# Expert stage of a decoder step: u and v rows gathered apart, v one pick to a partition and a tile later

## The chip, the cores and the metric

The kernel runs on one core of a Trainium2 chip. The metric is the device time of one execution in microseconds (us), the median of several runs.

## The reference, cut to what matters

One step of a hybrid decoder layer over 1024 prompt tokens and 32 sample tokens (8 sequences of 4), all in fp32. Sliding-window attention, a gated convolution and their merge come first. The change lies in the last part, the expert layer (PEER), on the normed rows h2 of width 1024:

```python
q = (tb @ w_pq).reshape(128, 8, 2, 128)                 # 8 heads, 2 halves
s = einsum('thpd,hpkd->thpk', q, sub_keys)              # 128 keys for each half
sv, si = top_k(s, 16)
cand = sv[:, :, 0, :, None] + sv[:, :, 1, None, :]      # 16 x 16 pairs
cs, ci = top_k(cand, 16)
e = i1 * 128 + i2                                       # 16 experts of 16384, a head and token
g = softmax(cs)
a = gelu(einsum('td,thkd->thk', tb, u[e]))
out = einsum('thkd,thk->td', v[e], g * a)
```

So each of 1056 tokens reads 128 rows of u and 128 rows of v (its picks), each row 1024 fp32 (4 KB), and y = x1 + gt2 * out.

## The kernel before, in words

The table uv holds u and v of an expert side by side (8 KB). In `peer_stage` tokens lie on partitions, in 8 tiles of 128 and a ninth of 32. A unit is one tile and one head: 16 picks for each token. The loops (`schedule`) run over tiles t and heads h, and each engine works through the same units in order.

- GpSimd (`unit`, L1501) issues 16 indirect gathers a unit. One gather fetches for pick j the uv row of each of the 128 tokens, 128 x 8 KB = 1 MB, into one of the 8 buffers of `ring`. It waits on `slot_free`, which TensorE raises when it has used the buffer.
- VectorE (`dots`, L1642) multiplies the u half with `h2c` and sums along the row, one pick an instruction. After each 4 picks it makes the gelu polynomial (L1645 to L1649), takes the tanh of ScalarE (L1521) and makes 4 coefficients (L1651, L1653).
- ScalarE (`weigh`, L1525) makes a 128 x 128 diagonal of each coefficient column.
- TensorE (L1589) multiplies each diagonal with the v half, in two chunks of 512 columns, into `acc`, over all 128 picks of a tile. An fp32 matmul is recorded as two passes, so a pick is 4 records.
- The choice of experts runs one tile (8 units) ahead: TensorE makes q (L1570), its transposes (L1575) and scores (L1581), ScalarE moves them (L1532), and VectorE takes the top 16 (`choose`, L1663 to L1690) and the ids and gates (`choose_ids`, L1700 to L1714). On VectorE `choose` stands behind the 16 dots of a unit.
- Before tile 0 stands a pass `tile(-1, ...)` with the choice for its 8 units. After tile 7 the 32 sample tokens are folded: their 128 picks lie on 4 groups of 32 partitions, so that two units of 16 gathers do them. `end` multiplies `acc` with gt2 and adds x1 (L1630, L1632).

## Time and profile before

| | |
|---|---|
| median of 3 runs | 4851.54 us (4840.93 to 4852.66) |
| span of the profiled execution | 4831.2 us |
| what the median run has over this span | 20.3 us |
| busy: TensorE, VectorE, ScalarE, GpSimd | 3823.7, 2615.1, 796.5, 1264.0 us |
| DMA, whole span | 1258.73 MB, mean 261 GB/s |

The span reaches from the first to the last instruction of the profiled execution; the time of a run counts what lies around it too, and the profiled execution has no time of its own beside its span. A granted TensorE clock of 1.00 is 2.4 GHz, 0.50 is 1.2 GHz. DMA share is the mean busy share of the core's 16 DMA engines. The expert stage takes the last two thirds of the span.

### The profile page before, as it was taken

To read this page: it belongs to the slowest core of one execution; us is meant where nothing else is said; L and a number is where in the kernel's file an instruction comes from. 1 tells how busy PE (TensorE), PEld (TensorE's weight loads), DVE (VectorE), ACT (ScalarE), POOL (GpSimd) and SP (SyncE) were. 2 spreads that over 40 slices of the span, in tenths; PEclk is the share of its full clock that TensorE was granted. 3 is DMA by queue.
4 is the path that set the end of the run, shared out by engine and by line. 5 is a ranking of instruction groups with operands and counts; after the bars stand their busy time and mean duration, and the time that the engine had idled before them with its cause. 6 is when DMAs were issued, how large, how long until landed. Compare 5 with 4: busy or idle time off the path is not lost.

```text
span 4831.2 us, 47220 instructions
## 1 busy us (share of the span) xinstructions
PE 3823.7 (79%) x12534; PEld 2194.0 (45%) x12534; DVE 2615.1 (54%) x6696; ACT 796.5 (16%) x2303; POOL 1264.0 (26%) x1255
## 2 busy tenths in 40 slices
PE   7788869999997677777777777777777777777776
PEld 1455559999963333333333333333333333333331
DVE  0344442223323766666666666666666666666655
ACT  0233321112001111111111111111111111111110
POOL 0111120000000133333333333333333333333333
PEclk9888859999998888888898988898999888988888
DMA  6100011111364588988898988898998898998887
GB/s 239 66 11 9 4 49 67 62 66 63 120 226 156 202 352 346 363 346 352 357 359 346 361 353 358 353 363 344 356 364 357 337 368 349 360 353 341 323 337 286
DMA packets 201700, 1258.73 MB, mean 261 GB/s; under 512 B 27375, under 2 KB 38367, under 8 KB 64479
## 3 DMA queue, kind: packets, MB, share of 16 engines
q0 software_dynamic: 152064, 1107.36, 57.8%
q1 hardware_dynamic: 49562, 150.46, 8.8%
q8 instruction: 36, 0.59, 0.0%
q14 instruction: 38, 0.31, 0.0%
HBM read 1226.81 MB, written 32.93 MB: 261 GB/s over the span
## 4 chain that ended last, share of the span: by engine, by line
PE 21%; DVE 20%; DMA 16%; issue 8%; ACT 1%; POOL 1%; DVEq 1%; POOLq 0%; SPq 0%
PE acc_peer L1589 20%; DMA rows<-in_uv,idx 16%; DVE rows L1642 5%; POOL rows L1501 1%; DVE pick L1700 1%; DVE pick L1703 1%; DVE picked L1705 1%; DVE key_scores_rest L1667 1%; DVE top_keys L1666 1%; DVE top_keys L1673 1%; DVE pair_scores_rest L1682 1%; DVE best_scores L1684 1%; DVE best_scores L1679 1%; DVE best_pairs L1687 1%; ACT tanh L1521 1%
## 5 line engine op out<-in xcount | busy, mean ns | idle before, releaser
L1589 PE MATMUL acc_peer<-rows,diag 128*128 128x512 f32 (+1 forms) x4224 | 2146.1, 667 | 764.5 <-ACT diag L1525 764.1
L1642 DVE CUSTOM_DVE_ANT_0 rows<-rows,h_now 128x1024 f32<-128x1024 f32 x1056 | 1268.3, 1224 | 926.5 <-DMA rows<-in_uv,idx 911.3
L1589 PEld LDWEIGHTS acc_peer<-rows,diag 128*128 128x128 f32 (+1 forms) x4224 | 873.2, 213 | 1923.4 <-issue 1877.3
L1501 POOL DMA_INDIRECT rows<-in_uv,idx x1056 | 1132.7, 1073 | 2064.9 <-PE acc_peer L1589 1916.7
L1521 ACT ACTIVATE tanh<-poly 128x4 f32<-128x4 f32 x264 | 54.2, 205 | 2180.4 <-DVE poly L1649 2180.4
L1525 ACT ACTIVATE diag<-ident,coef 128x128 f32<-128x128 f32 x1024 | 327.2, 390 | 110.2 <-DVE coef L1653 110.2
L880 PE MATMUL conv_bank<-hi_part,w_hi 128*128 128x352 f32 x960 | 310.6, 324 | 3.2 <-DVE w_lo L873 3.2
L880 PE MATMUL conv_bank<-h_lo,w_hi 128*128 128x352 f32 x960 | 308.6, 321 | 0.0
L880 PE MATMUL conv_bank<-hi_part,w_lo 128*128 128x352 f32 x960 | 308.4, 321 | 0.0
L1570 PE MATMUL ps_q<-wide,h2T_now 128*128 (+1 forms) x1152 | 281.6, 401 | 14.3 <-DMA sub_keys<-in_subkT 14.3
L1570 PEld LDWEIGHTS ps_q<-wide,h2T_now 128*128 128x128 f32 (+1 forms) x1152 | 221.6, 194 | 87.8 <-issue 47.7
L600 PE MATMUL psQ<-w_qkv,hTc 128*128 128x512 f32 (+1 forms) x432 | 214.3, 635 | 2.4 <-ACT hTc L342 2.4
L873 DVE TENSOR_TENSOR w_lo<-w_raw,w_hi 128x1024 fp32r<-128x1024 f32 x56 | 68.5, 1225 | 233.1 <-ACT w_hi L869 233.0
L880 PEld LDWEIGHTS conv_bank<-hi_part,w_hi 128*128 128x128 f32 x960 | 180.9, 188 | 3.3 <-issue 3.3
L880 PEld LDWEIGHTS conv_bank<-h_lo,w_hi 128*128 128x128 f32 x960 | 181.1, 189 | 0.0
L880 PEld LDWEIGHTS conv_bank<-hi_part,w_lo 128*128 128x128 f32 x960 | 180.6, 188 | 0.0
L1283 PE MATMUL psY<-w_out,mT 128*128 128x512 f32 (+1 forms) x288 | 127.6, 602 | 11.7 <-DMA mT<-merged_d 11.7
L600 PEld LDWEIGHTS psQ<-w_qkv,hTc 128*128 128x128 f32 (+1 forms) x432 | 77.4, 193 | 91.7 <-issue 88.3
L527 DVE SCALAR_TENSOR_TENSOR S<-psS,mask 128x1024 f32<-128x1024 f32 x32 | 39.2, 1225 | 137.5 <-PE psS L610 137.5
L1016 POOL COPY conv_new<-u 128x2 f32 (+1 forms) x8 | 1.5, 186 | 416.9 <-DVE u_s L1047 416.9
L869 ACT ACTIVATE w_hi<-w_raw 128x1024 fp32r<-128x1024 f32 x56 | 59.1, 1056 | 293.3 <-PE conv_bank L880 150.7
L182 PE MATMUL acc<-wide,csil 128*9 128x512 f32 x192 | 85.5, 603 | 15.5 <-DMA wide<-in_w_ada 15.5
(203 smaller groups left out, 3322.8 us busy)
## 6 DMA issues: line engine op xcount, KB each, us to landing
w_raw<-in_w_units SPq DMA_DIRECT2D x56, 512.0 KB, 3.5
wide<-in_w_ada SPq DMA_DIRECT2D x12, 2048.0 KB, 7.9
rows<-in_uv,idx POOLq DMA_INDIRECT x1056, 9.4
gates_d<-gate_tanh SPq DMA_DIRECT2D x16, 528.0 KB, 2.7
gate<-gates_d SPq DMA_DIRECT2D x16, 528.0 KB, 4.0
w_qkv<-in_w_qkv SPq DMA_DIRECT2D x3, 2048.0 KB, 18.0
merged_d<-merged SPq DMA_DIRECT2D x8, 528.0 KB, 5.3
x<-in_x SPq DMA_DIRECT2D x8, 512.0 KB, 3.3
```

Source lines behind the costliest of these rows:

```text
L182: mm = nc.tensor.matmul(acc[b][0:NR, :], csil[:, k, :], w[b][:, k, :], start=(k == 0), stop=(k == DK - 1))
L600: mm = nc.tensor.matmul(psQ[c % 2][0:rows, :], hTc[:, k, 0:rows], w_qkv[:, k, c * 512:(c + 1) * 512], start=(k == 0), stop=(k == DK - 1))
L869: nc.scalar.activation(self.hi[q][:], self.raw[q][:], ACT.Copy).then_inc(self.hi_ready, 1)
L873: nc.vector.tensor_tensor(self.lo[q][:], self.raw[q][:], self.hi[q][:].bitcast(F32), ALU.subtract).then_inc(self.lo_ready, 1)
L880: mm = nc.tensor.matmul(out, w[:, k, :], x[:, k, cols], start=(k == 0 and n == 0), stop=(k == DK - 1 and n == 2))
L1283: mm = nc.tensor.matmul(psY[b][0:rows, c * 512:(c + 1) * 512], mT[b][:, kk, 0:rows], w[:, kk, c * 512:(c + 1) * 512], start=(kk == 0), sto ...
L1501: nc.gpsimd.indirect_dma_start(ring[j % RING][:], None, d["uv"], bass.IndirectOffsetOnAxis(ap=idx[b][:, j:j + 1], axis=0)).then_inc(gather ...
L1521: nc.scalar.activation(th[bq][:], g1[bq][:], ACT.Tanh, scale=GELU_A).then_inc(tanh_done, 1)
L1525: nc.scalar.activation(diag[r][:, 0:NS] if last else diag[r][:], fold[:] if last else ident[:], ACT.Copy, scale=co[bq][:, k:k + 1]).then_i ...
L1570: mm = nc.tensor.matmul(psq[r, :], h2T[:, k, r], w[:, k, cols], start=(k == 0), stop=(k == DK - 1))
L1589: mm = nc.tensor.matmul(acc[out, c * 512:(c + 1) * 512], diag[j % RING][:, out], ring[j % RING][:, D + c * 512:D + (c + 1) * 512], start=F ...
L1642: nc.vector.tensor_tensor_reduce(u, u, h2c[r, :], 1.0, 0.0, ALU.mult, ALU.add, a[bq][r, k:k + 1]).then_inc(dotted, 1)
```

## The change

- The table is read as rows of u and rows of v: id 2e for u, 2e + 1 for v. `gather_u` fetches 128 x 4 KB for one pick of the 128 tokens, into 8 buffers `u_rows`, each free again after its dot. `gather_v` fetches the 128 v rows of one token, one pick to a partition, into 8 buffers `v_rows`. Both are issued from GpSimd in turn, v for the tile before.
- The ids and the coefficients of a tile (tokens on partitions, 128 picks along the row) are turned on TensorE once a tile (`turn_ids`, `turn_coef`). ScalarE writes the turned coefficients into `spread`, a mostly zero buffer, in which token n owns 32 columns with its coefficients in one of them.
- For one token the sum over picks is then a matmul with 128 x 32 weights into 32 output partitions, again 2 chunks of 512. Four tokens (`quad`) go to the four column groups of TensorE. The tile of 32 sample tokens lies in one group. The diagonals are gone.
- The gelu is done once for 16 picks. The choice runs 2 units ahead, with 2 units in front of the first dots.
- After the last dots of tile 7 come the choice for 6 units of the sample tile, the v gathers of tile 7, the folded sample units and the 32 v gathers of the sample tile.
- Loops are written out; one range of old semaphores is cleared in `conv_stage`.

```diff
+        RU, RV = 8, 8
-        ring = [m.sb(f"rows{r}", [P, 2 * D]) for r in range(RING)]
-        diag = [m.sb(f"diag{r}", [P, P]) for r in range(RING)]
+        u_rows = [m.sb(f"u_rows{r}", [P, D]) for r in range(RU)]
+        v_rows = [m.sb(f"v_rows{r}", [P, D]) for r in range(RV)]
...
+        acc = [m.ps(f"acc_peer{b}", [P, D]) for b in range(2)]
...
+        table = d["uv"].rearrange("e (a n) -> (e a) n", a=2)
...
+        def token(t, k):
+            return k if t == NT else NS * (k % 4) + k // 4
...
-                    hold(pool, slot_free, TOPK * n + j + 1)
-                    nc.gpsimd.indirect_dma_start(ring[j % RING][:], None, d["uv"],
-                                                 bass.IndirectOffsetOnAxis(ap=idx[b][:, j:j + 1], axis=0)).then_inc(gathered[j % RING], 16)
+            def gather_u(i, idx):
+                r = i % RU
+                if i >= RU:
+                    hold(pool, dotted, i - RU + 1)
+                nc.gpsimd.indirect_dma_start(u_rows[r][:], None, table, bass.IndirectOffsetOnAxis(ap=idx, axis=0)).then_inc(u_landed[r], 16)
+            def gather_v(t, k):
+                g = P * t + k
+                r = g % RV
+                if k == 0:
+                    hold(pool, idsT_ready, t + 1)
+                if g % 4 == 0 and g >= RV:
+                    hold(pool, quads_done, g // 4 - RV // 4 + 1)
+                n = token(t, k)
+                nc.gpsimd.indirect_dma_start(v_rows[r][:], None, table, bass.IndirectOffsetOnAxis(ap=idsT[t % 2][:, n:n + 1], axis=0)).then_inc(v_landed[r], 16)
+            for n in range(UT):
+                t, h = divmod(n, PH)
+                hold(pool, ids_ready, n + 1)
                 for j in range(TOPK):
+                    gather_u(TOPK * n + j, ids[t % 2][:, h * TOPK + j:h * TOPK + j + 1])
+                    if t:
+                        gather_v(t - 1, h * TOPK + j)
+            HALF = P // 2
+            for k in range(HALF):
+                gather_v(NT - 1, k)
+            hold(pool, folded, 32 * FOLDS)
+            for j in range(2 * TOPK):
+                gather_u(TOPK * UT + j, ids_s[:, j // TOPK, j % TOPK:j % TOPK + 1])
+                gather_v(NT - 1, HALF + j)
+            for k in range(HALF + 2 * TOPK, P):
+                gather_v(NT - 1, k)
+            for k in range(NS):
+                gather_v(NT, k)
...
+            def move_scores(k):
+                r = slice(0, rows_of(k))
+                move(q_sb[r, :], psq[r, :], q_mult, k + 1, q_moved)
+                move(qT[:, :, r], psT[:, :, r], q_turned, k + 1, qT_moved)
+                if k:
+                    act.wait_ge(top_step, TOP * k)
+                move(sc[r], pss[r], key_mult, k + 1, keys_moved)
...
+            def spread_coef(t):
+                act.wait_ge(x_turned, 2 * t + 2)
+                if t >= 2:
+                    act.wait_ge(quads_done, quads_before(t - 1))
+                n = 1 if t == NT else P // NS
+                dst = spread[t % 2][:].rearrange("p (j x) -> p j x", x=NS * NS)[:, 0:n, 0:NS * NS:NS + 1]
+                nc.scalar.activation(dst, psX[:, 0:n * NS].rearrange("p (j x) -> p j x", x=NS), ACT.Copy).then_inc(spread_ready, 1)
...
+            for n in range(UT):
+                t, h = divmod(n, PH)
+                if h == 6:
+                    move_ids(t)
+                if h == 0 and t:
+                    spread_coef(t - 1)
+                move_scores(n + 2)
+                tanh_of(n)
+                softmax_of(n + 2)
+                if h == 5:
+                    cast_ids(t)
+            spread_coef(NT - 1)
...
-                            hold(pe, diag_ready, TOPK * n + j + 1)
-                            for c in range(2):
-                                out = slice(0, NS if last else P)
-                                mm = nc.tensor.matmul(acc[out, c * 512:(c + 1) * 512], diag[j % RING][:, out],
-                                                      ring[j % RING][:, D + c * 512:D + (c + 1) * 512], start=False, stop=False, skip_group_check=True)
-                            mm.then_inc(slot_free, 1)
...
+            def quad(t, q):
+                if q == 0:
+                    pe.wait_ge(spread_ready, t + 1)
+                    if t >= 2:
+                        pe.wait_ge(y_ready, t - 1)
+                for k in range(4 * q, 4 * q + 4):
+                    g = P * t + k
+                    pe.wait_ge(v_landed[g % RV], 16 * (g // RV + 1))
+                last = (NS if t == NT else P) // 4 - 1
                 for c in range(2):
+                    for k in range(4 * q, 4 * q + 4):
+                        n = token(t, k)
+                        at = n // NS * NS
+                        if t == NT:
+                            first, end = k == 0, k == NS - 1
+                        else:
+                            first, end = q == 0, q == last
+                        mm = nc.tensor.matmul(acc[t % 2][at:at + NS, c * 512:(c + 1) * 512], spread[t % 2][:, n * NS:(n + 1) * NS],
+                                              v_rows[(P * t + k) % RV][:, c * 512:(c + 1) * 512], start=first, stop=end)
+                mm.then_inc(quads_done, 1)
+            for k in range(2):
+                query(k)
+                turn_query(k)
+                score(k)
+            for n in range(UT):
+                t, h = divmod(n, PH)
+                query(n + 2)
+                if h == 6:
+                    turn_ids(t)
+                if h == 0 and t:
+                    turn_coef(t - 1)
+                if t:
+                    quad(t - 1, 4 * h)
+                turn_query(n + 2)
+                if t:
+                    quad(t - 1, 4 * h + 1)
+                score(n + 2)
+                if t:
+                    quad(t - 1, 4 * h + 2)
+                    quad(t - 1, 4 * h + 3)
+            turn_coef(NT - 1)
+            for k in range(UT + 2, KT):
+                query(k)
+                turn_query(k)
+                score(k)
+                quad(NT - 1, k - UT - 2)
+            turn_ids(NT)
+            for q in range(6, P // 4):
+                quad(NT - 1, q)
+            turn_coef(NT)
+            for q in range(NS // 4):
+                quad(NT, q)
...
+            def finish(t):
+                r = slice(0, NS if t == NT else P)
+                dve.wait_ge(gt2_loaded, 16 * (1 + DEC_B) if t == NT else 16)
+                dve.wait_ge(quads_done, quads_before(t) + (NS if t == NT else P) // 4)
+                dve.wait_ge(x1_loaded, 16 * (t + 1))
+                nc.vector.tensor_tensor(acc[t % 2][r, :], acc[t % 2][r, :], gt2[r, :], ALU.mult).then_inc(y_step, 1)
+                dve.wait_ge(y_step, t + 1)
+                nc.vector.tensor_tensor(x1[r, :], acc[t % 2][r, :], x1[r, :], ALU.add).then_inc(y_ready, 1)
+            for k in range(2):
+                choose(k)
+                gate(k)
+            for n in range(UT):
+                t, h = divmod(n, PH)
+                dots(n)
+                gelu_poly(n)
+                if h == 0 and t >= 2:
+                    finish(t - 2)
+                choose(n + 2)
+                gelu_end(n)
+                gate(n + 2)
+            for k in range(UT + 2, KT):
+                choose(k)
+                gate(k)
+            finish(NT - 2)
+            dve.wait_ge(folded, 32 * FOLDS)
+            for n in range(UT, UT + 2):
+                dots(n)
+                gelu_poly(n)
+                gelu_end(n)
+            finish(NT - 1)
+            finish(NT)
```

## Rows read from the trace of the kernel before

**Rows 1.** Windows: us, engines' busy time (count), clock, DMA share and GB/s.

```profile
2500.00:3000.00 500.00, 384.22 (x900) 182.03 (x900) 324.13 (x911) 76.14 (x262) 182.54 (x178) 0.88 0.89 353
3016.00:3032.00 16.00, 11.04 (x32) 6.29 (x31) 14.62 (x42) 2.15 (x8) 4.08 (x5) 0.85 1.00 420
3032.00:3036.00 4.00, 4.00 (x8) 1.61 (x7) 2.61 (x9) 0.49 (x2) 1.02 (x1) 0.73 0.09 18
```

**Rows 2.** Waits, 1900 to 4700 us: engine, whom it waited for, us, times, longest.

```profile
POOL rows L1501 <- PE acc_peer L1589: 1660.7, 683, 17.8
DVE rows L1642 <- DMA rows<-in_uv,idx: 785.3, 454, 5.0
```

**Rows 3.** The chain that ended last: two of its longest pieces, ten units apart.

```profile
2951.55 12.04 DMA rows<-in_uv,idx
...
3431.99 12.22 DMA rows<-in_uv,idx
```

**Rows 4.** Timeline: start us, us, engine, line; the first two dots.

```profile
1629.02 1.22 DVE L1642 CUSTOM_DVE_ANT_0 rows<-rows,h_now 128x1024 f32<-128x1024 f32 x1 [0.20 <-DVE gates_now L1725]
...
1630.17 1.22 DVE L1642 CUSTOM_DVE_ANT_0 rows<-rows,h_now 128x1024 f32<-128x1024 f32 x1
```

**Rows 5.** Timeline: last small step of a gelu, the next dot, one choice's first and last.

```profile
3003.46 0.16 DVE L1653 TENSOR_TENSOR coef<-coef,gates_now 128x4 f32<-128x4 f32 x1
...
3003.65 1.23 DVE L1642 CUSTOM_DVE_ANT_0 rows<-rows,h_now 128x1024 f32<-128x1024 f32 x1
...
3013.53 0.49 DVE L1663 MAX8 top_scores<-key_scores 128x8 f32<-128x128 f32 x2
...
3022.64 0.37 DVE L1714 TENSOR_SCALAR half_gates<-exp_best,exp_rsum 128x16 f32 x1
```

**Rows 6.** Timeline of GpSimd's gathers behind the fold, and the dot beside one.

```profile
4729.96 0.94 POOL L1501 DMA_INDIRECT rows<-in_uv,idx  x1 [0.31 <-issue]
4731.20 0.94 POOL L1501 DMA_INDIRECT rows<-in_uv,idx  x1 [0.30 <-issue]
...
4735.66 1.23 DVE L1642 CUSTOM_DVE_ANT_0 rows<-rows,h_now 128x1024 f32<-128x1024 f32 x1 [7.48 <-DMA rows<-in_uv,idx]
4736.17 1.53 POOL L1501 DMA_INDIRECT rows<-in_uv,idx  x1 [0.30 <-issue]
```

**Rows 7.** All gathers by line: duration ns min/median/max, and time to landing.

```profile
L1501 POOL DMA_INDIRECT rows<-in_uv,idx x1056: 932/937/1978, 1561.4 to 4805.2; - x176
...
DMA to landing us min/median/max: 5.2/9.4/16.3
```

**Rows 8.** DMA view of 806 to 812 us: one load of 128 rows of 4 KB.

```profile
GB/s 0 0 0 0 0 0 0 0 0 0 0 0 0 0 109 246 82 82 0 164 273 437 410 437 437 355 328 109 27 0 0 0 0 0 0 0 0 0 0 0
DMA packets 144, 0.52 MB, mean 87 GB/s; under 512 B 16, under 2 KB 16, under 8 KB 144
...
q1 hardware_dynamic: 144, 0.52, 30.9%
...
w_raw<-in_w_units SPq DMA_DIRECT2D x1, 512.0 KB, 3.5
```

**Rows 9.** TensorE timeline: two groups of 16 passes, a query, 128 x 32 weights.

```profile
3021.13 3.62 PE L1570 MATMUL ps_q<-wide,h2T_now 128*128 x16
...
3029.70 9.32 PE L1589 MATMUL acc_peer<-rows,diag 128*128 128x512 f32 x16 [4.96 <-ACT diag L1525]
...
3039.07 7.03 PE L1589 MATMUL acc_peer<-rows,diag 128*128 128x512 f32 x16
...
4824.03 0.11 PEld L1589 LDWEIGHTS acc_peer<-rows,diag 128*32 128x32 f32 x1 [0.32 <-issue]
4824.46 0.11 PEld L1589 LDWEIGHTS acc_peer<-rows,diag 128*32 128x32 f32 x1 [0.32 <-issue]
```

**Rows 10.** The end of the span, timeline.

```profile
4826.43 1.21 DVE L1630 TENSOR_TENSOR y_out<-acc_peer,gt 32x1024 f32<-32x1024 f32 x1 [7.56 <-PE acc_peer L1589]
...
4828.92 0.33 SPq L1480 DMA_DIRECT2D out_y<-y_out  x1
```

More of the change, by code:

```diff
@@ L1413, in peer_stage @@
+        quads_done, folded, unfolded, y_step, y_ready = s("quads_done"), s("folded"), s("unfolded"), s("y_step"), s("y_ready")
         block = ctx.enter_context(nc.Block())
[L1414 removed]
         FOLDS = P // NS
[L1418 to L1439 removed]
+        TOP = 19
@@ L1593, in tile @@
-            def tile(t, rows, next_rows):
-                if next_rows:
-                    pe.wait_ge(h2T_loaded, 16 * (t + 2))
-                if rows:
-                    begin(t, rows)
-                with pe.Fori(0, PH // 2) as hp:
-                    for b in range(2):
-                        unit(PH * t + 2 * hp + b, 2 * hp + b, b, rows, next_rows, False)
-            tile(-1, None, P)
-            with pe.Fori(0, NT - 1) as t:
-                tile(t, P, P)
-            tile(NT - 1, P, NS)
@@ L1606, in _, with query @@
-            begin(NT, P)
-            for b in range(2):
-                unit(PH * NT + b, b, b, P, None, True)
+            pe.wait_ge(small_loaded, 32)
+            def query(k):
+                r = slice(0, rows_of(k))
+                h = k % PH
+                if h == 0:
+                    pe.wait_ge(h2T_loaded, 16 * (k // PH + 1))
+                if k:
+                    pe.wait_ge(q_moved, k)
+                for c in range(DK):
+                    mm = nc.tensor.matmul(psq[r, :], h2T[:, c, r], w[:, c, h * 2 * PHALF:(h + 1) * 2 * PHALF], start=(c == 0), stop=(c == DK - 1))
+                mm.then_inc(q_mult, 1)
@@ L1655, in choose, with dots @@
-            def choose(m_, h, rows):
-                r = slice(0, rows)
-                one = bass.ds(h, 1)
-                st = Steps(dve, top_step, base=TOP * m_, own=True)
+            dve.wait_ge(small_loaded, 32)
+            SMALL = 4
+            def dots(n):
+                t = n // PH
+                if n % PH == 0:
+                    dve.wait_ge(h2_loaded[t % 2], 16 * (t // 2 + 1) if t < NT else 16 * (NT // 2 + FOLDS))
+                for j in range(TOPK):
+                    i = TOPK * n + j
+                    r = i % RU
+                    dve.wait_ge(u_landed[r], 16 * (i // RU + 1))
+                    nc.vector.tensor_tensor_reduce(u_rows[r][:], u_rows[r][:], h2[t % 2][:], 1.0, 0.0, ALU.mult, ALU.add, a[n % 2][:, j:j + 1]).then_inc(dotted, 1)
@@ L1732, in _ @@
-            schedule(dve, unit, begin, end)
+                st.wait()
+                pk = Steps(dve, pick_step, base=4 * k)
+                pk.did(nc.vector.tensor_tensor(pick[r].rearrange("p a k j -> p (a k) j"), bc(pair[r].rearrange("p a k -> p (a k)").unsqueeze(2), [rows, 2 * TOPK, TOPK]),
+                                               bc(iota[r, :].unsqueeze(1), [rows, 2 * TOPK, TOPK]), ALU.is_equal))
+                pk.wait()
+                pk.did(nc.vector.tensor_tensor(pick[r], pick[r], bc(topf[r].unsqueeze(2), [rows, 2, TOPK, TOPK]), ALU.mult))
@@ L1736, in build @@
+            for n in range(UT, UT + 2):
+                dots(n)
[3 more added lines that the diff above has]
+            finish(NT)
 def build(nc, ins, outs):
```

411 lines of the change are left out of this document (189 added, 222 removed).

## The prediction

> **What bounds the kernel now.** I read the windows by stretch first. In the middle of the expert stage no engine is full: of 500 us TensorE is busy 384, VectorE 324, GpSimd 183, and the DMA engines stand at a share of 0.89 with 353 GB/s [rows 1]. Narrower windows show why the mean is under 1: for 16 us the share is 1.00 at 420 GB/s, then for 4 us it is 0.09 [rows 1]. The queue runs dry once a unit. The waits name the ring: GpSimd waited 1660.7 us in 683 waits for TensorE to free a slot, 17.8 us at worst, and then VectorE waits for rows (785.3 us) [rows 2]. A slot of 8 KB is held until its dot, gelu, diagonal and matmuls are done, and during a choice (9.5 us on VectorE, 3013.53 to 3023.01 [rows 5]) no slot can come free once the old coefficients are used up. The chain gives the price: ten units from 2951.55 to 3431.99 us, so 48.0 us a unit [rows 3], where 16.8 MB at 420 GB/s would take 40.0. So the loss to attack is 8 us a unit, and the floor under it is the DMA rate.
>
> **The front.** First dots are at 1629.0 [rows 4], behind eight choices. With two, six choices of 9.5 us go: first dots at 1572.
>
> **Tile 0 after.** Only u is fetched. VectorE needs 16 dots at 1.15 us (1629.02 to 1630.17 [rows 4]) = 18.4, a choice 9.5, five small gelu instructions at 0.2 (0.19 from one small step's start to the next instruction [rows 5]) = 1.0: 28.9 us. GpSimd needs 16 x 1.24 = 20 and the DMA 8.4 MB, 20 us, so VectorE sets it: 8 x 28.9 = 231 us, to 1803. In tiles 1 to 7 these 28.9 us lie beside the gathers; so do the ids' and coefficients' turns, the casts and the 2.4 us of `finish`, once in 8 units, as long as the gathers are the longer. The diagonals and 15 of 20 small gelu steps a unit leave engines that don't set the end: 0 us.
>
> **Tiles 1 to 7: GpSimd issues twice as often.** A unit now has 32 gathers of 128 rows. Issued freely, they follow each other in 1.24 us (4729.96 to 4731.20: 0.94 + 0.30 [rows 6]), and I keep 0.94 for a gather of half rows, since the count of rows is the same. That is 39.8 us a unit, the lower bound. The median gather of the whole trace is as short, 937 ns, but the longest is 1978 [rows 7]: one that starts inside a dot waits for its end. The dot 4735.66 ends at 4736.89; the gather that starts at 4736.17 ends at 4737.70, 0.81 behind it [rows 6]. A start at a random point of a dot costs on average half of 1.23 + 0.81 = 1.42 in place of 0.94, so 0.48 more. If all 32 paid it: 1.72 us each, 55.0 a unit, the upper bound. I walk through a unit. In 10.5 us without dots GpSimd issues 8.4 gathers, 4.2 pairs. Then dots run back to back at 1.15 and the gathers fall in with them at about 1.2; a backlog of 4.2 pairs, filled at one per 2.4 us, is gone in 4.2 / (1/1.15 - 1/2.4) = 9.3 us, in which 3.9 pairs come. The other 7.9 dots start as their rows land; a dot covers one of the pair's two starts about 9 times in 10, so a pair takes 2.49 + 0.9 x 0.48 = 2.92 us: 23.1. Sum 42.9, and 0.6 for a tile's loads and stores (about 2 MB in 8 units): 43.5 us.
>
> The DMA side: a load of 128 rows of 4 KB reached 437 GB/s at its height, but 0.52 MB took 30.9% of 16 engines over 6 us, 1.85 us, standing alone [rows 8]. With up to 16 gathers in flight I take the saturated 420 [rows 1], 1.25 us a gather, 40.0 a unit and 0.6 of other traffic. The other end, 1.85, is 59 us a unit.
>
> The page "DMA: Bandwidth & Descriptors" of the Trainium skill (Rules for kernel authors; Bandwidth) speaks against the change: it asks for at least 1 MiB a DMA, and its fit, 2.0 us + bytes / 436e3, gives 3.2 us for half a MiB. An estimate by that page, were gathers not overlapped, is 32 x 3.2 = 102 us a unit.
>
> **TensorE** makes 32 matmuls for v a unit, as before, 64 passes. Passes with 128 x 32 weights in one column group follow each other in 0.43 us (4824.03 to 4824.46), as those of 128 x 128 do (16 in 7.03, and 9.32 where the clock was partly low) [rows 9]. A quad has 16 passes: 6.9 us if nothing overlaps, 1.7 if four groups run abreast. No row shows passes in different groups. I take 3.8, two at a time, since the passes of one matmul wait for each other. With a query of 3.6 [rows 9] and some 2 for turns and scores, TensorE has 21 us (33 without overlap) in 43.5; at half clock all of it doubles. A v slot is asked for again five pairs (13.6 us) after the last issue of its quad, and is free after landing (about 4.5) and 3.8: enough. Behind a late quad stand the next v gather, and u too, as GpSimd issues in order.
>
> The page "TensorEngine Tiling (Array Packing)" (Theoretical Speedup) promises up to 4x for four column tiles; by it a quad takes 1.7 us and the sum below falls by 14 us, all in the tail.
>
> Sum of tiles 1 to 7: 56 x 43.5 = 2436, to 4239.
>
> **The tail.** v lags a tile, so 192 gathers of half size remain. (a) Turns and spread, 4 us, then six choices, 57; each of six quads stands behind a choice's turns on TensorE, so only 32 gathers go out: 61 us. (b) Where v goes alone, two quads are in flight: 3.7 us to issue four, 4.0 to land (5.2 at least for 1 MB [rows 7], less 1.2 for half of it), 0.2 and the quad, for two quads. With 3.8 that is 5.9 a quad, 16 quads: 94. The 8 quads of the sample tile lie in one column group, 6.9: 7.4 each, 59. (c) 32 u and 32 v in turn: 64 x 1.36 = 87. (d) Last landing, quad, two VectorE steps of 1.21, store (4826.43 to the span's end is 4.8 now [rows 10]): 20. Sum 321, where now 136 lie behind unit 64 (1629 + 64 x 48.0 = 4701, less 6 for a fast start). To 4560.
>
> **Forecast.** A span of 4560 us, 271 less than 4831.2. The median run is 20.3 above that execution's span, and I keep that: 4580 us. Of the gain, 57 are the front, 153 tile 0 (231 for 384), 252 the 56 units, and about 190 are given back in the tail. Chance 0.58, for 42 to 45.5 us a unit 4490 to 4700.
>
> **Rivals.**
> 1. The DMA rate alone sets the unit. For it: the free issue of 1.24 is as fast as 420 GB/s needs. Against: a gather started in a dot pays. 40.6 a unit, v quads at issue pace (16 x 5.0 + 59), the mixed part 80: 1803 + 2274 + 300 = 4377, run 4397. Chance 0.10.
> 2. The four column groups don't overlap. For it: passes of 32 columns now take as long as those of 128 [rows 9]. Against: 33 us still fit beside the gathers; but 6.9 + 4.5 of 13.6 leaves little, and at half clock nothing. 46 a unit, 24 quads at 7.4, tail 349: 1803 + 2576 + 349 = 4728, run 4748. Chance 0.15.
> 3. Slower: GpSimd's issue becomes the bound. Place: gathers queued behind dots, in every unit. It decides from 48.3 us a unit ((4831 - 1803 - 325) / 56), 1.51 us a gather; at 1.6, 51.2 a unit: 1803 + 2867 + 336 = 5006, run 5026. For it: a start in a dot costs 1.72 with its gap [rows 6]. Against: dots fill 18.4 of 43.5 us. Chance 0.12.
> 4. Slower: gathers of half size don't fill the engines; at 1.85 us [rows 8] 59 a unit, 1803 + 3321 + 377 = 5501, run 5521. Against: 437 GB/s in the middle of one lone load. This is also how the DMA page's rule would come out here. Chance 0.05.
>
> The range 4380 to 4800 holds the forecast, rivals 1 and 2, and leaves out 3 and 4 and some edges. A measurement of this kernel tells about 0.3% (15 us) from no change: slower 0.17 (rivals 3, 4), same 0.03 (the top of rival 2), faster 0.80.
>
> **What would show it.** First dots near 1572; tile 0 at 29 us a unit with VectorE full; then 43.5 us a unit with GpSimd busy some three quarters and hardly waiting for anyone, a DMA share over 0.9; gathers with a mean of 1.0 to 1.1 us; quads of 3.8 us. A DMA share of 1.00 speaks for rival 1, quads of 6.9 for 2, a mean gather over 1.2 for 3, a full share at a low rate for 4. The forecast is wrong if GpSimd waits on `quads_done` or `dotted` in every unit, or if the tail is far from 321 us.

## The result, and the profile after

The change made the kernel slightly slower. The median is 4867.3 us (4 runs, 4865.0 to 4872.7) against 4846.2 us for the kernel before on the same chip (4 runs, 4836.8 to 4852.7): a ratio of 1.0055 with a 95% interval of 1.0036 to 1.0073. The forecast was 4580 us, in a range of 4380 to 4800. Now and then an execution is slow as a whole (one of nine of the kernel before, in a later comparison, took 5427.2 us at a mean clock of 0.65), so the ratios here leave such ones out, while runs 1 to 9 below are one execution each.

The profiled execution has a span of 4870.7 us. Windows of it (us, then busy time and count of TensorE, its weight loads, VectorE, ScalarE, GpSimd, then clock, DMA share, GB/s), the first as in [rows 1]:

```profile
2500.00:3000.00 500.00, 204.65 (x898) 71.76 (x898) 298.98 (x754) 20.28 (x70) 372.49 (x333) 0.65 0.96 352
...
3116.00:3120.00 4.00, 3.39 (x16) 0.69 (x16) 3.79 (x22) 0.22 (x1) 3.16 (x3) 0.50 1.02 417
3132.00:3136.00 4.00, 0.00 (x0) 0.00 (x0) 4.00 (x9) 0.00 (x0) 3.39 (x3) 0.50 0.85 269
```

The loss that was to be won back is still there, and it looks different now. The transfers ran at 353 GB/s with a share of 0.89 before, with a hole of nearly nothing once a unit [rows 1]. Now they run at 352 GB/s with a share of 0.96, with no hole but with stretches of 269 GB/s. TensorE's busy time is nearly halved (384 to 205 us in 500), and its granted clock is 0.65 in place of 0.88. GpSimd has doubled, 183 to 372 us, and with 0.30 us ahead of each of 333 gathers (100 us) it has under 30 us left.

The groups of GpSimd's instructions from 2200 to 4200 us (busy us, mean ns, idle time before them and what ended it):

```profile
L1520 POOL DMA_INDIRECT v_rows<-in_uv,v_ids x663 | 764.9, 1154 | 299.8 <-issue 194.5 <-DMA wide<-in_w_ada 104.7 <-PE acc_peer L1681 0.6
L1510 POOL DMA_INDIRECT u_rows<-in_uv,u_ids x663 | 726.7, 1096 | 209.9 <-issue 200.5 <-DVE dots L1731 9.1 <-PE acc_peer L1681 0.3
```

Where [rows 2] had GpSimd waiting 1660.7 us for TensorE, it hardly waits for anyone now, except for 104.7 us that the profile puts down to a transfer that ended long ago (run 5 comes back to them). These are 41 units of 48.3 us. Each is 32 gathers of 1.125 us, 32 pauses of 0.30 to 0.31 (36 and 9.8 us), and 2.5 us of longer waits, nearly all ahead of the first v gather of a quad.

By the forecast's own stretches, in us:

| | kernel before | forecast | measured |
|---|---|---|---|
| first dots | 1629.0 | 1572 | 1568.8 |
| tile 0 (8 units) | 385.8 | 231 | 257.6 |
| tiles 1 to 7 (56 units) | 2721 (48.6 each) | 2436 (43.5 each) | 2695 (48.1 each) |
| from there to the end | 95.5 | 321 | 349 |
| span | 4831.2 | 4560 | 4870.7 |

So 259 of the 311 us that the forecast missed lie in the 56 units. Against the kernel before, the front and tile 0 win 188 us, the 56 units win 26, and the longer tail gives back 254. The timeline shows where a large part of the 259 us goes: GpSimd first, then VectorE, in the same stretch.

```profile
3131.35 1.98 POOL L1520 DMA_INDIRECT v_rows<-in_uv,v_ids  x1 [0.30 <-issue]
3133.64 1.99 POOL L1510 DMA_INDIRECT u_rows<-in_uv,u_ids  x1 [0.30 <-issue]
3135.93 1.99 POOL L1520 DMA_INDIRECT v_rows<-in_uv,v_ids  x1 [0.30 <-issue]
```
```profile
3131.30 1.23 DVE L1731 CUSTOM_DVE_ANT_0 u_rows<-u_rows,h_now 128x1024 f32<-128x1024 f32 x1
...
3132.44 1.23 DVE L1731 CUSTOM_DVE_ANT_0 u_rows<-u_rows,h_now 128x1024 f32<-128x1024 f32 x1
...
3133.59 1.23 DVE L1731 CUSTOM_DVE_ANT_0 u_rows<-u_rows,h_now 128x1024 f32<-128x1024 f32 x1
```

Dots follow each other in 1.145 us, gathers in 2.29 us, exactly two dots. A gather that starts inside a dot ends 0.81 us behind that dot's end [rows 6]: here the dot of 3131.30 ends at 3132.53 and the gather at 3133.33. With 0.30 of pause the next gather starts at 3133.64. By then not the next dot but the one after it has begun (3133.59), and the gather waits for that one's end. The two engines lock in step, and the gathers come at half the dots' rate. The window 3132:3136 is what this does to the transfers: 269 GB/s.

The Trainium skill's page "SBUF — State Buffer" (SBUF: two separate sides) describes an exclusive lock on the port pair that VectorE and GpSimd share: an instruction of VectorE with two inputs in SBUF keeps out a GpSimd instruction that reads SBUF, for its whole length. This trace agrees, in that the gather is held to the end of the dot and ends 0.81 us later. The same page of the Trainium skill (Who interferes with whom) reports that `tensor_tensor` did not stall DMAs that GpSimd issues. Here the measurement decides otherwise for indirect gathers: they are held by instructions of that kind too (see run 1).

### The profile page after: what moved, and what is told of

Same layout as the page of the kernel before. It is cut to its first block, busy times and chain, and to the rows that moved or that the text cites. A ratio compares the mean times of both kernels' runs of the same rounds, so it can differ in the third digit from the quotient of the medians.

```text
span 4870.7 us, 37283 instructions
## 1 busy us (share of the span) xinstructions
PE 2723.5 (56%) x12534; PEld 1535.7 (32%) x12534; DVE 2423.6 (50%) x5631; ACT 441.8 (9%) x1076; POOL 2493.4 (51%) x2246
## 4 chain that ended last, share of the span: by engine, by line
POOL 43%; issue 13%; DVE 4%; DMA 4%; another core or an unknown queue 3%; PE 2%; ACT 0%; SPq 0%; POOLq 0%; DVEq 0%; ACTq 0%
POOL v_rows L1520 22%; POOL u_rows L1510 21%; DMA v_rows<-in_uv,v_ids 2%; PE acc_peer L1681 2%; DMA u_rows<-in_uv,u_ids 1%; DVE u_rows L1731 1%; DVE pick L1797 0%; DVE pick L1800 0%; DVE picked L1802 0%; PE ps_q L1625 0%; DVE top_keys L1776 0%; DVE top_keys L1769 0%; DVE key_scores_rest L1770 0%; DVE top_scores L1773 0%
## 5 line engine op out<-in xcount | busy, mean ns | idle before, releaser
L1681 PE MATMUL acc_peer<-v_rows,coef_spread 128*32 128x512 f32 x4224 | 954.6, 1007 | 1632.7 <-DMA v_rows<-in_uv,v_ids 1605.3
L1731 DVE CUSTOM_DVE_ANT_0 u_rows<-u_rows,h_now 128x1024 f32<-128x1024 f32 x1056 | 1265.1, 1224 | 1064.3 <-DMA u_rows<-in_uv,u_ids 922.3
L1520 POOL DMA_INDIRECT v_rows<-in_uv,v_ids x1056 | 1193.4, 1130 | 544.8 <-issue 302.0
L1510 POOL DMA_INDIRECT u_rows<-in_uv,u_ids x1024 | 1151.2, 1124 | 379.8 <-issue 308.0
L1681 PEld LDWEIGHTS acc_peer<-v_rows,coef_spread 128*32 128x32 f32 x4224 | 187.2, 153 | 2163.2 <-issue 2156.0
L1625 PE MATMUL ps_q<-wide,h2T_now 128*128 128x256 f32 (+1 forms) x1152 | 307.9, 427 | 13.5 <-DMA sub_keys<-in_subkT 13.5
L1625 PEld LDWEIGHTS ps_q<-wide,h2T_now 128*128 128x128 f32 (+1 forms) x1152 | 233.5, 209 | 152.6 <-issue 110.3
L1634 PE MATMUL ps_qT<-ident,q_sb 128*128 128x128 f32 (+1 forms) x144 | 42.0, 387 | 205.9 <-ACT q_sb L1547 153.7
L1564 ACT ACTIVATE tanh<-poly 128x16 f32<-128x16 f32 x66 | 14.3, 216 | 1347.7 <-DVE poly L1741 783.2
L1634 PEld LDWEIGHTS ps_qT<-ident,q_sb 128*128 128x128 f32 (+1 forms) x144 | 18.6, 181 | 301.6 <-ACT q_sb L1547 174.9
```

Of the source, the lines that this page charges most:

```text
L1510: nc.gpsimd.indirect_dma_start(u_rows[r][:], None, table, bass.IndirectOffsetOnAxis(ap=idx, axis=0)).then_inc(u_landed[r], 16)
L1520: nc.gpsimd.indirect_dma_start(v_rows[r][:], None, table, bass.IndirectOffsetOnAxis(ap=idsT[t % 2][:, n:n + 1], axis=0)).then_inc(v_landed ...
L1564: nc.scalar.activation(th[n % 2][:], g1[n % 2][:], ACT.Tanh, scale=GELU_A).then_inc(tanh_done, 1)
L1625: mm = nc.tensor.matmul(psq[r, :], h2T[:, c, r], w[:, c, h * 2 * PHALF:(h + 1) * 2 * PHALF], start=(c == 0), stop=(c == DK - 1))
L1634: mm = nc.tensor.transpose(psT[:, p, r], q_sb[r, p * P:(p + 1) * P], ident[r, r])
L1681: mm = nc.tensor.matmul(acc[t % 2][at:at + NS, c * 512:(c + 1) * 512], spread[t % 2][:, n * NS:(n + 1) * NS], v_rows[(P * t + k) % RV][:, ...
```

## The experiments

Where an experiment has a time a unit, it is the mean of units 16 to 56, which are tiles 2 to 6. Runs 2, 3, 5, 6, 7 and 9 also clear the buffers first, so that their first dots come some 15 us later.

**1. Dots with one input.** The product with h2 is left out, so the dot is a plain sum of the u row.

```diff
-nc.vector.tensor_tensor_reduce(u_rows[r][:], u_rows[r][:], h2[t % 2][:], 1.0, 0.0, ALU.mult, ALU.add, a[n % 2][:, j:j + 1])
+nc.vector.tensor_reduce(a[n % 2][:, j:j + 1], u_rows[r][:], AX, ALU.add)
```

> The changed kernel, but VectorE's dot is a sum of the u row alone (tensor_reduce, one SBUF input); the product with h2 is left out. Theory I (GpSimd's issue stream sets a unit of tiles 1 to 7: 32 gathers of 1.13 us, longer than 0.94 only where they start in a dot, 0.30 us between them, and 2.6 us of stalls = 48.3): every gather takes 0.94, 32 x 1.24 + 2.6 = 42.4 us a unit, or, if the DMA engines' time of 45.8 us a unit then binds, 45.8 to 46.5 at a share of 1.0; span 4730 to 4760, or 4530 at 42.4. Theory D (the DMA engines alone bind at 4 KB rows): 47.5 to 48.3 as now.

Measured: 4733.1 us, 46.2 us a unit. Its windows and GpSimd's groups, 2200 to 4200 us:

```profile
2200.00:4200.00 2000.00, 849.16 (x3740) 304.24 (x3740) 1224.38 (x2454) 77.66 (x277) 1310.08 (x1386) 0.65 0.97 370
```
```profile
L1510 POOL DMA_INDIRECT u_rows<-in_uv,u_ids x693 | 658.6, 950 | 213.2 <-issue 191.5 <-DVE dots L1731 21.6
L1520 POOL DMA_INDIRECT v_rows<-in_uv,v_ids x693 | 651.7, 940 | 477.1 <-DMA wide<-in_w_ada 259.1 <-issue 197.7 <-DVE dots L1731 12.1
```

With one input no gather is held (0.95 us, as when free), although VectorE is as busy as before. The edit also takes away the dot's wide output, but that is not the cause, as two other steps of VectorE in the changed kernel show. Each writes 1024 columns, the second of them into SBUF, and has only one input in SBUF, the other in PSUM, and the gathers that start inside them are as short as free ones:

```profile
3019.82 1.23 DVE L1822 TENSOR_TENSOR acc_peer<-acc_peer,gt 128x1024 f32<-128x1024 f32 x1
3021.09 1.22 DVE L1824 TENSOR_TENSOR x_now<-acc_peer,x_now 128x1024 f32<-128x1024 f32 x1
```
```profile
3020.37 0.94 POOL L1510 DMA_INDIRECT u_rows<-in_uv,u_ids  x1 [0.30 <-issue]
3021.61 0.94 POOL L1520 DMA_INDIRECT v_rows<-in_uv,v_ids  x1 [0.30 <-issue]
```

In that trace 14 gathers start well inside these two steps and none takes over 0.95 us, while all 24 that start well inside the choice's `pick` products, with both inputs in SBUF, take 1.08 to 1.38. So the hold needs the second input in SBUF. It is worth 32 x 0.18 = 5.7 us a unit, but only 2.1 of them are kept: GpSimd's longer waits, again ahead of v gathers, rise from 2.5 to 6.2 us a unit. The transfers stand at 0.97 and 370 GB/s, which is 381 at a share of 1.00. At that rate 16.8 MB would take 44.0 us, an estimate. The forecast's 420 GB/s was not reached over a unit: the best 48 us of this run, 3680 to 3728, moved 399 GB/s.

**2 and 3. Half of each row.** Only 2 KB of each u and v row are fetched; run 3 has the one-input dots as well.

```diff
-table = d["uv"].rearrange("e (a n) -> (e a) n", a=2)
+table = d["uv"].rearrange("e (a n) -> (e a) n", a=4)
-indirect_dma_start(u_rows[r][:], None, ...
+indirect_dma_start(u_rows[r][:, 0:D // 2], None, ...
```

> The changed kernel, but each gather fetches 2 KB of a row (half the bytes; same gathers, dots and matmuls, so the rest of each buffer is zero). Theory I: the unit stays at 47.5 to 48.5 us with a DMA share near 0.6. Theory D: under 45 us. If both bind about equally, 46 to 47.5.

> Both edits: row sums in place of dots, and half of each row fetched. Theory I: 32 x 1.24 + 2.6 = 42.4 us a unit, whatever the DMA. If e1 gives 46 and this 42.4, the engines' time at 4 KB rows is a second bound just under the issue. Theory D: far under 42, down to VectorE's 29 to 33.

Measured: 4872.4 us and 48.29 us a unit for run 2, the same as the changed kernel to 0.1%, with half of the bytes. Run 3: 4692.7 us, 45.7 a unit. The window of run 2:

```profile
2200.00:4200.00 2000.00, 806.73 (x3571) 285.60 (x3572) 1180.26 (x2989) 76.37 (x263) 1596.22 (x1326) 0.64 0.62 180
```

The transfers are at 0.62 and nothing is gained, so the changed kernel is bound by GpSimd's issue and not by bytes. In run 2 no wait over a microsecond is left: its gathers are 1.21 us on average, and 32 x (1.21 + 0.30) = 48.3. In run 3 the gathers are short (0.96) and 5.4 us of waits a unit stand nearly all ahead of v gathers, with a DMA share of 0.64. My theory of two causes asked for 42.4 us a unit there. It fell, and these waits became the question.

**4. The split alone, in the kernel before.** Each slot's uv row comes in two gathers of 4 KB rows in place of one of 8 KB.

```diff
+for half in range(2):
+    nc.gpsimd.indirect_dma_start(ring[j % RING][:, half * D:(half + 1) * D], None, table,
+        bass.IndirectOffsetOnAxis(ap=idx[b][:, half, j:j + 1], axis=0)).then_inc(gathered[j % RING], 16)
```

> The kernel before with one edit: each slot's 8 KB gather is made as two gathers of 4 KB rows (u, then v), the same ids, slots, dots and diagonals. It prices the split alone. If DMA packets of 4 KB cost 179 ns against 330 of 8 KB as in the two traces, the engines need 45.8 in place of 42.3 us a unit, and the dry spell once a unit stays: 51 to 53 us, span 5050 to 5150. If the split costs nothing, 48.0 us and span 4831.

Measured: 5331.0 us, against 4844.0 before: 10% slower, 55.2 us a unit in place of 48.05, with a share of 0.84 at 308 GB/s. Both of my forecasts (51 to 53 us a unit, or 48.0) were too low. Splitting each gather in two costs 487 us in this kernel. Some 0.9 us a unit of it are GpSimd's second row of ids, and the choice on VectorE took 14.1 us in place of 9.0, which run 6 takes up. The rest of the change (slots free after the dot, no diagonals, a shorter front) gives back all of it but some 20 us.

**5. More v buffers.** The waits of run 3 stood at gathers that wait for the quad that last used their buffers. The trace's record of the semaphore's count shows that these were real waits for that quad: in the changed kernel a quad ended at 3120.25 by its modelled end, the count moved at 3124.75, and the v gather started at 3125.01. In 36 of the 40 such waits of units 16 to 56 the count moved 0.2 to 0.3 us ahead of the gather. The modelled end itself is good: in the tail, where v gathers go alone and wait for each quad, they start 0.29 us behind it (the quad of 4789.57, 3.64 us long, ends at 4793.21).

```profile
4793.50 0.94 POOL L1520 DMA_INDIRECT v_rows<-in_uv,v_ids  x1 [4.14 <-PE acc_peer L1681]
```

So the question was why the quads' word came late. Run 5 is run 3 with sixteen v buffers of 512 columns:

```diff
-RU, RV = 8, 8
+RU, RV = 8, 16
-v_rows = [m.sb(f"v_rows{r}", [P, D]) for r in range(RV)]
+v_rows = [m.sb(f"v_rows{r}", [P, D // 2]) for r in range(RV)]
```

> The changed kernel with 2 KB of each row gathered and dots of one input (as in e3), and 16 v buffers of 512 columns in place of 8 of 1024; a quad reads the same 512 columns for both halves. In e3 GpSimd stood still 5.4 us a unit, each time just ahead of the first v gather of a quad, which waits for the quad that freed its buffers, and each time the count of done quads moved 0.26 us before the gather started. Theory A (v buffers): eight v buffers are two quads, too few for landing, PE's turn and the quad; with sixteen the waits go, a unit is 32 x 1.25 = 40.1 us and the time near 4692 - 56 x 5.4 = 4390 us. Theory B (a path that GpSimd's descriptors share with the semaphores is full, a floor near 1.43 us a gather whatever the buffers): the waits come back elsewhere, a unit stays at 45 to 46 us and the time at 4650 to 4700.

Measured: 4866.4 us, 49.0 a unit. GpSimd's groups:

```profile
L1513 POOL DMA_INDIRECT u_rows<-in_uv,u_ids x653 | 617.4, 946 | 567.9 <-DVE dots L1736 400.7 <-issue 167.2
L1523 POOL DMA_INDIRECT v_rows<-in_uv,v_ids x652 | 616.5, 945 | 198.6 <-issue 196.5 <-PE acc_peer L1685 2.1
```

The waits for quads are gone, as theory A had it, and a single wait of 9.3 us a unit, for a u buffer and so for VectorE's dots, took their place. The kernel became slower, which neither theory had foreseen; that the wait came back elsewhere is theory B's.

**6. And a dot of 16 elements.** Run 5 with a dot that sums 16 elements, so that VectorE has little to do but the choice.

```diff
-nc.vector.tensor_reduce(a[n % 2][:, j:j + 1], u_rows[r][:], AX, ALU.add)
+nc.vector.tensor_reduce(a[n % 2][:, j:j + 1], u_rows[r][:, 0:16], AX, ALU.add)
```

> e5 with a dot that sums only the first 16 elements of the u row: VectorE has next to nothing to do for a pick. Theory A: as e5, 40 us a unit, about 4390 us, since one-input dots did not lengthen a gather. Theory B (floor near 1.43 us a gather): 45 to 46 us a unit, as e3. If VectorE's own work is what holds the semaphores back, this one falls well under e5.

Measured: 4792.3 us, 48.25 a unit, above the 45 to 46 of theory B and far from the 40 of A. The timeline of VectorE within one choice, then of TensorE within one quad beside it:

```profile
3024.21 0.48 DVE L1771 MAX8 top_scores<-key_scores 128x8 f32<-128x128 f32 x2
...
3032.04 0.18 DVE L1786 TENSOR_SCALAR top_keys_f<-top_keys 128x32 f32<-128x32 uint32 x1 [4.68 <-remote]
3034.84 0.09 DVE L1789 MATCH_VALUE_LOAD best_pairs<-best_scores,pair_scores 128x8 f32 x1 [2.29 <-remote]
3040.44 0.43 DVE L1792 MAX8 best_scores<-pair_scores_rest 128x8 f32<-128x256 f32 x1 [4.72 <-remote]
3046.04 0.17 DVE L1797 TENSOR_SCALAR pair_halves<-best_pairs 128x16 uint32<-128x16 uint32 x1 [4.34 <-remote]
...
3049.62 0.17 DVE L1811 SCALAR_TENSOR_TENSOR u_ids<-picked 128x16 uint32<-128x16 f32 x1
```
```profile
3036.93 0.67 PE L1685 MATMUL acc_peer<-v_rows,coef_spread 128*32 128x512 f32 x1 [0.99 <-issue]
3039.74 1.01 PE L1685 MATMUL acc_peer<-v_rows,coef_spread 128*32 128x512 f32 x1 [2.14 <-issue]
3042.53 1.01 PE L1685 MATMUL acc_peer<-v_rows,coef_spread 128*32 128x512 f32 x1 [1.78 <-issue]
```

The choice takes 25.6 us, with four stalls of 2.3 to 4.7 us. Each stalled step waits for nothing but an earlier step of VectorE itself. TensorE meanwhile does one matmul in 2.8 us. GpSimd had by then issued gathers 1.25 us apart without a break for over 20 us. The same stalls, smaller, are in the changed kernel:

```profile
3121.18 0.18 DVE L1781 TENSOR_SCALAR top_keys_f<-top_keys 128x32 f32<-128x32 uint32 x1 [1.00 <-DVE pair_scores L1777]
...
3124.75 0.43 DVE L1787 MAX8 best_scores<-pair_scores_rest 128x8 f32<-128x256 f32 x1 [1.94 <-remote]
```

VectorE went on at 3124.75, the very moment at which the late quad's count moved. So it is not one quad that is late: the updates of several engines come late together. I call this the lag. Two more signs belong to it. Once a quad has begun, TensorE's matmuls wait for no semaphore, and in run 6 they come one by one all the same, so the lag is not in semaphores alone. And the trace loses part of its semaphore records: of the 1368 steps of the choice it has all in the kernel before, 1347 in run 9 below, 884 in run 2, 782 in the changed kernel and 774 in run 6.

**7 to 9. Gathers further apart.** A memset on GpSimd behind every gather, which the next memset waits for: 128 x 1 on run 6 (run 7) and on the changed kernel (run 8), and 128 x 512 on run 6 (run 9).

```diff
+def pad():
+    if pads[0]:
+        hold(pool, padded, pads[0])
+    nc.gpsimd.memset(spare[:], 0.0).then_inc(padded, 1)
+    pads[0] += 1
```

> e6 with one small memset on GpSimd behind every gather, waited for, so that gathers start some 1.45 to 1.6 us apart and not 1.25. In e6 a unit took 48.25 us: 32 gathers at 0.947 + 0.303 = 40.0 and one wait of 8.5 us for a u buffer, which came free late because in the stretches of unbroken gathers VectorE, TensorE and ScalarE stood for 2 to 5 us at steps that wait for a semaphore. Theory B (a stream of gathers 1.25 us apart is more than the shared path of descriptors and semaphores takes, and the other engines' semaphores pay): spread out, the stalls on VectorE and the 8.5 us wait go, and a unit is 32 x the spacing, 46 to 51 us, near e6 or below. Theory C (the wait is simply VectorE's choice, 9.5 us long, behind a ring of eight): the wait stays at 8 us less what the slower walk covers, 32 x 0.25 = 8 us of cover, so a unit of 48 to 51 too, but VectorE's stalls inside the choice stay at 2 to 5 us. What tells them apart is the length of the choice: about 9.5 us by B, 20 and more by C.

> The changed kernel with the same memset behind every gather. Theory B with GpSimd's issue as the bound: the 2.5 us of waits a unit go, the pads come on top: 48.3 - 2.5 + 32 x (0.2 to 0.3) = 52 to 55.5 us a unit, and 4867 + 56 x 4 to 7 = 5090 to 5270 us. Rival (DMA at its own rate is the bound, and GpSimd's walk has slack): a unit stays at 48.3 and the time near 4870.

> e7 with a memset of 128 x 512 in place of 128 x 1 (some 0.5 to 0.6 us). In e7 the small memset (0.12 us) fell inside the 0.30 us that lies between two gathers anyway, so gathers still started 1.25 us apart, and VectorE's choice still stood 2 to 4.5 us at each of four steps; GpSimd's own memset was waited for too, 138 us in 2,000. If the lag of the semaphores comes with gathers that start 1.25 us apart, gathers 1.6 to 1.75 us apart are without it: the stalls inside the choice go, and a unit is 32 x 1.6 to 1.75 = 51 to 56 us, set by GpSimd alone (5000 to 5250 us). If it comes with the number of gathers under way, which the ring sets, the stalls stay and the unit is longer still.

Run 7: 4673.4 us, 45.9 a unit. Run 8: 4860.6 us, 47.6 a unit. GpSimd's groups of run 8 show why it became no slower:

```profile
L1529 POOL DMA_INDIRECT v_rows<-in_uv,v_ids x672 | 774.9, 1153 | 192.1 <-issue 130.7 <-DMA wide<-in_w_ada 59.8 <-PE acc_peer L1691 1.1
L1518 POOL DMA_INDIRECT u_rows<-in_uv,u_ids x672 | 739.2, 1100 | 141.2 <-issue 126.7 <-DVE dots L1741 14.0
L1511 POOL MEMSET spare<- 128x1 f32 x1343 | 158.7, 118 | 0.4
```

The memset (0.12 us) fits into the 0.30 us that pass between two gathers anyway: 0.19 are left beside it. So the gathers were not spread, and my expectation of run 8 rested on a pad that cost something; 5090 to 5270 us did not come, and this run says little of GpSimd's slack. In run 7 the choice still took 22.5 us, and GpSimd's own memsets waited 138 us in 2000 for the memset before. I had named a choice of 20 us and more as the sign of theory C, but with gathers still 1.25 us apart the run tests neither. Why the small memset makes run 7 faster than run 6 (45.9 against 48.25 us a unit), and shortens the choice of run 8, no run shows.

Run 9 spreads them. VectorE in one choice, then GpSimd's groups:

```profile
3009.49 0.48 DVE L1781 MAX8 top_scores<-key_scores 128x8 f32<-128x128 f32 x2
...
3014.23 0.43 DVE L1802 MAX8 best_scores<-pair_scores_rest 128x8 f32<-128x256 f32 x1
...
3018.22 0.17 DVE L1821 SCALAR_TENSOR_TENSOR u_ids<-picked 128x16 uint32<-128x16 f32 x1
```
```profile
L1514 POOL MEMSET spare<- 128x512 f32 x1206 | 652.3, 541 | 0.6
L1521 POOL DMA_INDIRECT u_rows<-in_uv,u_ids x603 | 576.8, 957 | 99.6 <-issue 99.6
```

With gathers 1.66 us apart the choice takes 8.9 us, and from 2200 to 4200 us no step of VectorE but a dot waits over 0.3 us. A unit is 53.1 us (5106.8 us in all), 32 x 1.66, set by GpSimd alone. The choice, from its first step to the ids, is the measure of the lag. These are medians of the units from 2200 to 4200 us, beside the distance from one gather's start to the next:

| | rows | mean distance, us | share under 1.3 us | choice, us |
|---|---|---|---|---|
| before | 8 KB | 3.00 | 2% | 9.0 |
| changed | 4 KB | 1.51 | 64% | 11.1 |
| run 1 | 4 KB | 1.44 | 91% | 11.8 |
| run 2 | 2 KB | 1.51 | 55% | 8.3 |
| run 3 | 2 KB | 1.43 | 91% | 12.1 |
| run 4 | 4 KB | 1.73 | 69% | 14.1 |
| run 5 | 2 KB | 1.53 | 97% | 23.8 |
| run 6 | 2 KB | 1.50 | 97% | 25.4 |
| run 7 | 2 KB | 1.44 | 83% | 22.5 |
| run 8 | 4 KB | 1.49 | 65% | 8.4 |
| run 9 | 2 KB | 1.66 | 0% | 8.9 |

The lag comes with gathers 1.25 us apart, and most of all in a long row of them: in runs 5 and 6, with sixteen v buffers, GpSimd stops once a unit. In run 2 the rows are short, mostly two gathers and some six in the choice, and no step of the choice waits. The changed kernel has the same mean distance as run 2 but whole rows, and there some of the lag is left. Run 8 differs from it only by the memset and has less: a median of 8.4 us, though single choices still take up to 13.

**10 to 12. Another cure for the kernel before.** By the prediction's reading it lost its time because no slot came free during 9.5 us of choice, and the queue ran dry. Run 10 writes the loop over heads out (the control), run 11 also cuts the choice into four parts, one behind each batch of four dots, and makes it one unit later. Run 12 puts TensorE's weighted adds ahead of the query's work.

```diff
-with eng.Fori(0, PH // 2) as hp:
+for hp in range(PH // 2):
...
 for q in range(NB):
-    dots(n, b, q, rows)
-if next_rows:
-    choose(m_, h, next_rows)
-    choose_ids(m_, h, next_rows, rows is not None)
+    if rows:
+        dots(n, b, q, rows)
+    if parts:                 # choose(m_ - 1, ...) as a generator, in four parts
+        next(parts)
```

> The kernel before with the loop over pairs of heads written out (a tile is eight units of code in one loop over tiles); nothing else changes. Control for the next run. If written-out code costs nothing: 4844 us within 0.3%. If every engine's instruction fetch stands in the way of the gathers: some 0.5 to 1 us a unit, 4875 to 4910.

> f1 with the choice of a unit cut in four parts, one behind each batch of four dots, and made one unit later (unit n chooses for unit n + 7). The gathers stay 8 KB a pick, one a pick. Theory (the kernel before lost its DMA time because 9.5 us of choice let the eight buffers fill): the share rises from 0.89 toward 0.97, a unit falls from 48.0 to 42 to 43.5 us, and the time to 4844 - 64 x 5 = 4520 us (4480 to 4580). Rival (the row buffers are held back by PE's or ScalarE's turn, not by the choice): 4780 to 4850. Rival (dots and gathers meet more often when spread): GpSimd's gathers lengthen to 1.4 us and more, but 16 x (1.4 + 0.8) = 35 us stays under 42, so no price.

> The spread choice (g1), with TensorE doing the four weighted adds of a batch ahead of the query, transposes and scores of that quarter, not behind them. GpSimd waited 1040 us of 2000 for TensorE to free a buffer in g1, and the share of the transfers was 0.94. If the query's 3.6 to 9 us in front of the first batch held buffers back: share to 0.96 or more, 4640 to 4665 us. If TensorE has done the query before the first batch's weights come (rival): 4660 to 4690, no change from g1's 4675; if ScalarE now waits for the query ahead of the next batch's weights: slower, 4700.

Measured: run 10 4841.8 us, ratio 1.0001 (0.9991 to 1.0011). Run 11 4675.5 us against 4839.8, ratio 0.9664 (0.9648 to 0.9679). Run 12 4684.1 us, ratio 0.9685 (0.9665 to 0.9705): its interval overlaps that of run 11, and from 2200 to 4200 us both have a share of 0.94, so the order of TensorE's work makes no difference that was measured. Run 11's window, the first of [rows 1]:

```profile
2500.00:3000.00 500.00, 392.68 (x946) 187.26 (x946) 343.62 (x971) 78.09 (x275) 206.06 (x187) 0.91 0.95 374
```

The share rose from 0.89 to 0.95, a unit fell from 48.05 (48.8 in run 10's trace) to 46.2 us, and this version beats both kernels: it is 3.4% faster than the one before, where the change is 0.55% slower. It is less than the 42 to 43.5 us a unit that I expected. GpSimd's waits, 2200 to 4200 us:

```profile
POOL rows L1502 <- PE acc_peer L1602: 1039.8, 427, 18.3
POOL rows L1502 <- issue: 118.0, 257, 3.5
```

GpSimd still waits for free slots, and 374 GB/s at 0.95 is 394 at a share of 1.00, not 420. Where the rest of the expected gain went, no run shows.

## Why the prediction was wrong, point by point

- **What bounds the kernel before** was right: the dry queue during the choice. Run 11 fills part of that hole and gains 164 us. But 48.0 us a unit, read from ten units, is not the mean of the 56 (48.6), and 95.5 us lie behind unit 64, not 136. This leaves the forecast of the changed kernel alone; it shifts the gain between units and tail.
- **The front** was right, 1568.8 for 1572.
- **Tile 0** was forecast as VectorE's, 28.9 us a unit. It took 32.2: in the burst of dots the gathers are held there too (1.35 us on average), and of the 258 us VectorE waits some 30 for rows. The same step as the next.
- **The step that failed** is in "GpSimd issues twice as often": "dots run back to back at 1.15 and the gathers fall in with them at about 1.2". They fall in at 2.29, one for two dots. The prediction had the two numbers (0.81 behind the dot's end, 0.30 of pause) and averaged over a random start, where they make a fixed step. The prediction's walk, at 42.9 us, has room for 3.2 us of hold a unit; measured are 32 x (1.125 - 0.94) = 5.9. The other part of the miss are the longer waits, 2.5 us a unit, for which the walk had nothing but its 0.6 for other traffic. Together this is 2.7 + 1.9 = 4.6 us a unit, the difference from 43.5 to 48.1.
- **The second step that failed** is behind those waits: "A v slot ... is free after landing (about 4.5) and 3.8: enough". The quad took what was forecast (3.64), but it started 6.4 us after its last gather had (the median; 4.0 with half rows in run 2), and where GpSimd waited for it, the v gather mostly started 4.2 to 6.1 us behind the quad's end, against 0.29 in the tail. That this lag comes with gathers 1.25 us apart is shown by runs 6 and 9. It would also say why taking the hold away (run 1) gains 2.1 us a unit and not 5.7: the hold had kept the gathers apart.
- **The DMA term**, 420 GB/s for gathers of 4 KB rows, was too good: 381 GB/s by run 1. It did not decide, since run 2 with half of the bytes is as slow. Whether it would hold the unit at 44.0 us with the other two costs gone is an estimate that no run tests.
- **Rival 3** is what happened. It was to decide from 48.3 us a unit, and the kernel landed next to that point, at 48.1. With the tile 0 and the tail that were measured, the point lies at 47.4, and so the change costs 0.55%. Its chance, 0.12, came from the same mean over random starts. Against it I put that dots fill 18.4 of 43.5 us; where they run back to back, a gather comes not every 1.2 us but every 2.29. The mean gather alone (1.125 us) would not have told it by the sign that I named, "over 1.2".
- **Rival 2** fell. The tail has both kinds of quads, first one in four column groups, then one of the sample tile in a single group:

```profile
4789.57 3.64 PE L1681 MATMUL acc_peer<-v_rows,coef_spread 128*32 128x512 f32 x16 [6.67 <-DMA v_rows<-in_uv,v_ids]
4794.65 7.03 PE L1681 MATMUL acc_peer<-v_rows,coef_spread 128*32 128x512 f32 x16 [1.20 <-DMA v_rows<-in_uv,v_ids]
```

  The 3.64 us are at a clock of 0.50 (as in the window 3116:3120) and the 7.03 at 1.00, so the 16 passes overlap nearly four times (14.06 / 3.64 = 3.9), and my 3.8 was right by luck: I had two at a time at full clock. The page "TensorEngine Tiling (Array Packing)" of the Trainium skill (Theoretical Speedup) has up to 4x, and this case, with 3.9, agrees with it. TensorE was never the bound, and its clock fell with its work.
- **Rivals 1 and 4** fell with run 2. The Trainium skill's page "DMA: Bandwidth & Descriptors" (Rules for kernel authors) asks for at least 1 MiB a DMA, and this case agrees with its direction: halving the gathers costs 10% in run 4, and the rate at a share of 1.00 is 381 GB/s with rows of 4 KB (run 1) where run 11 has 394 with rows of 8 KB. The 3.2 us a gather that the prediction worked out for gathers one by one did not come: they overlap, and started 1.51 us apart.
- **The tail** took 349 us for 321. The 64 v gathers behind the choices for the sample tile took 130 us, from 4506.5 to 4637.0, where the forecast has 108; the folded part took 92 for 87, the last 32 v gathers of tile 7 56 for 47. Where v goes alone, a quad came every 6.9 us in place of 5.9: it starts 6.1 to 7.0 us after its last gather has, where the forecast had 4.2.
- **The 20.3 us** that were added to the span were not there: the profiled execution took 4872.7 us, 2.0 over its own span, and the other three lie below it. By this the 20.3 us of the kernel before are a difference between executions.

What stays open: what the lag is. No run shows which resource is short, how long a row of gathers it takes, and what their distance, their bytes and their number under way have each to do with it. Run 9 changed the distance and with it the number under way, and the changed kernel and run 2 differ in bytes alone but for the cleared buffers, yet the one has 2.5 us of waits a unit and the other none. A rival was not tested: the profiler writes records of its own, many of them are missing where gathers are close together, and no execution with a lag is known to have run without it. So how much of the lag an unprofiled execution has is not shown. The hold behind the dots does not hang on this, since it does not need the lag: run 2 has none and is as slow.

## What to carry to other kernels

Before you ask an engine to issue twice as often, walk its issue beside the neighbour that can hold it as a fixed step and not as a mean: take where the held one ends, add its pause, and see whether the next start falls inside a later instruction of the neighbour. A wait that is removed by a mechanism that doubles instructions (one gather for two) is easily paid back in full; here moving a quarter of the choice behind each batch of dots took part of the same hole at no extra gather. When steps that wait only for their own engine stand for microseconds, look at who issues gathers at that time, and try that engine slower.
